# Two-block transformer kernel on one core: the second block's values are multiplied ahead of its norm, and the gates' weights follow the units

## The reference, cut to what matters

```
def rmsnorm(x, g):
    y = x * rsqrt(mean(x * x, axis=-1) + EPS)
    return y * g

h = rmsnorm(x, norm_g)
proj = h @ w_in
aq, ak, av, az, bqk, bv, bi, bf, bo, bz, ga, gb = split(proj)
q = rope(rmsnorm(two_map_heads(aq), q_norm_g), cos, sin)
k = rope(rmsnorm(two_map_heads(ak), k_norm_g), cos, sin)
v = av                                   # the attention's values
...
return x + u @ w_o                       # the x of the next layer
```

## Time and profile before

| | |
|---|---|
| median of 3 runs | 1798.98 us (1798.03 to 1799.15) |
| the profiled execution | 1797.98 us, span 1796.1 us |
| TensorE busy in the span | 1731.1 us, 96% |
| mean granted TensorE clock | 0.984 of full speed |
| VectorE, ScalarE, GpSimd busy | 63%, 51%, 26% |

### The profile page before, as it was taken

How to read it: one execution, slowest core, us unless ns; L and a number is a source line. 1 busy time by engine, 2 the same in 40 slices (tenths; PEclk the granted TensorE clock), 3 DMA queues, 4 the chain that set the end, 5 groups by cost and what they waited for, 6 DMA issues and landing times.

```text
span 1796.1 us, 29026 instructions
## 1 busy us (share of the span) xinstructions
PE 1731.1 (96%) x10836; PEld 1433.7 (80%) x10836; DVE 1127.6 (63%) x2007; ACT 924.6 (51%) x1968; POOL 459.8 (26%) x864
## 2 busy tenths in 40 slices
PE   6999998999999999988999989999999899999998
PEld 3453566888888876557999988899899898998998
DVE  4228866888878333685555577686556675785555
ACT  3237653525252523674555565575554564664542
POOL 1016001000000020320000134067771161287730
PEclk9999999999999998998999999999999999999999
DMA  9323332455555321202554443524345335433351
GB/s 341 139 94 122 135 120 94 141 187 188 188 188 188 141 74 47 95 1 94 188 187 175 171 147 124 196 99 142 136 142 187 142 107 199 144 127 141 120 193 42
DMA packets 127541, 255.28 MB, mean 142 GB/s; under 512 B 2462, under 2 KB 7212, under 8 KB 127404
## 3 DMA queue, kind: packets, MB, share of 16 engines
q1 hardware_dynamic: 126406, 251.16, 39.3%
q0 software_dynamic: 704, 2.10, 0.4%
q10 hardware_dynamic: 294, 0.18, 0.0%
HBM read 252.38 MB, written 1.05 MB: 141 GB/s over the span
## 4 chain that ended last, share of the span: by engine, by line
PE 51%; DVE 1%; ACT 1%; issue 0%; POOL 0%; DVEq 0%; ACTq 0%
PE ps L1189 12%; PE ps L1191 12%; PE ps L1190 12%; PE ps L1436 2%; PE ps L1434 2%; PE ps L1435 2%; PE ps L1514 1%; PE ps L1517 1%; PE ps L1509 1%; PE ps L1090 1%; PE ps L1063 1%; PE ps L1480 1%; PE ps L1204 0%; PE ps L1205 0%; ACT big_r L1623 0%; DVE big_r L2091 0%
## 5 line engine op out<-in xcount | busy, mean ns | idle before, releaser
L2091 DVE TENSOR_TENSOR big_r<-ring,big_r 128x1024 fp32r<-128x1024 f32 x214 | 263.9, 1233 | 249.3 <-ACT big_r L1623 249.2
L1623 ACT ACTIVATE big_r<-ring 128x1024 fp32r<-128x1024 f32 x214 | 226.2, 1058 | 370.8 <-PE ps L1191 358.3
L1190 PE MATMUL ps<-big_r 128*128 128x256 f32 (+1 forms) x1088 | 360.6, 331 | 0.0
L1189 PE MATMUL ps<-hT_r,big_r 128*128 128x256 f32 (+1 forms) x848 | 270.6, 319 | 0.0
L1191 PE MATMUL ps<-hT_r,big_r 128*128 128x256 f32 (+1 forms) x848 | 265.6, 313 | 0.0
L1189 PE MATMUL ps<-big_r 128*128 128x256 f32 (+1 forms) x720 | 239.9, 333 | 1.4 <-DVE big_r L2277 1.4
L1191 PE MATMUL ps<-big_r 128*128 128x256 f32 (+1 forms) x720 | 237.9, 330 | 0.0
L930 POOL TENSOR_TENSOR sq<-sq 128x256 f32<-128x256 f32 (+1 forms) x30 | 36.1, 1202 | 730.4 <-ACT sq L1583 730.2
L1190 PEld LDWEIGHTS ps<-big_r 128*128 128x128 f32 x1088 | 206.8, 190 | 18.7
L1191 PEld LDWEIGHTS ps<-hT_r,big_r 128*128 128x128 f32 x848 | 161.5, 190 | 9.6
L1189 PEld LDWEIGHTS ps<-hT_r,big_r 128*128 128x128 f32 x848 | 161.6, 191 | 9.3 <-issue 0.2
(11 more groups left out here) (319 smaller groups left out, 4280.7 us busy)
## 6 DMA issues: line engine op xcount, KB each, us to landing
ring<-in_w_in SPq DMA_DIRECT2D x44, 2048.0 KB, 7.7
ring<-in_w_mlp SPq DMA_DIRECT2D x32, 2048.0 KB, 7.9
ring<-in_w_mod SPq DMA_DIRECT2D x24, 2048.0 KB, 8.0
ring<-in_w_out SPq DMA_DIRECT2D x4, 2048.0 KB, 9.0
ring<-in_w_out_a SPq DMA_DIRECT2D x4, 2048.0 KB, 7.8
ring<-in_w_out_b SPq DMA_DIRECT2D x4, 2048.0 KB, 7.8
ring<-in_w_o SPq DMA_DIRECT2D x4, 2048.0 KB, 7.8
ring<-in_w_in SPq DMA_DIRECT2D x2, 1152.0 KB, 11.0
```

The lines of the kernel that those rows point to most:

```text
L1189: mm(b[:, 0:T], w_hi[:, k, :], hi(k), start=(j == 0), stop=False)
L1190: mm(b[:, 0:T], w_hi[:, k, :], lo(k), start=False, stop=False)
L1623: act_fn(hi, raw, ACT.Copy).then_inc(hi_ready, 1)
L2091: V.tensor_tensor(lo, raw, hi.bitcast(F32), ALU.subtract).then_inc(lo_ready, 1)
```

## The change

In each layer of the second block, `av` is moved from behind the units to the very start. Its left operand is no longer the normed `h` but `x * g` in two rounded parts (`g_hi` made by `gained` on ScalarE, `g_lo` by `gained_rest` on VectorE, chunk by chunk as the last product of the layer before updates `xT`). Each token's root is brought from a row to a column by two transposes on TensorE (bank key `roots`) and a small copy, and multiplies the values when ScalarE copies them out of PSUM. The sum of squares comes behind the first of the eight `av` granules, the transposes behind the fifth. The splitting of granules 3 to 7 is woven into the chunk loop of the norm on both engines. The tail behind the units is now the two granules of `bif` and the first of `bv`. The order of slots, the banks of `av` and two buffers of the granules follow. No matmul of the products is added or removed.

```
@@ plan_banks @@
     for l in range(DEPTH):
         tag = ("b", l)
+        for n in range(4):
+            take((tag, "av", n), (2 if n // 2 == l else 6) + n % 2)
         take((tag, "lam"), 5)
         take((tag, "n1"), 4)
+        take((tag, "roots"), 5)
         unit_plan(tag, units_b())
-        for n in range(4):
-            take((tag, "av", n), n)
         for n in range(4):
             take((tag, "bv", n), n)
         take((tag, "bif"), 4)
-BEFORE = ("aq", "ak", "av", "bif", "bv")
+BEFORE = (("av", 0), ("av", 1), ("aq", 0), ("aq", 1), ("ak", 0), ("ak", 1), ("bif", 0), ("bv", 0), ("bv", 1))
...
@@ TensorE @@
+                for n, m in [(n, m) for n in range(2) for m in range(4)]:
+                    if n == 0:
+                        pe.wait_ge(g_ready, KC * l + 2 * m + 2)
+                    tokens_granule("av", n, m, g_hi[l], g_lo[l])
+                    if (n, m) == (0, 0):
+                        summed_squares((tag, "n1"), SEQ)
...
+                    if (n, m) == (1, 0):
+                        key = (tag, "roots")
+                        b = start_bank(key)
+                        pe.wait_ge(nt_ready, nt_before[l] + 1)
+                        for t in range(2):
+                            last = tr(b[:, t * P:(t + 1) * P], rstd[:, root_slot[l], t * P:(t + 1) * P], IDENT)
+                        fill(last, key)
...
-                run_units(tag, units_b(), main, [lambda m=m: tokens_granule("av", 0, m) for m in range(B_BUFS)])
-                tokens_product("av", B_BUFS)
...
+                run_units(tag, units_b(), main, [lambda: gates_granule(0), lambda: gates_granule(1),
+                                                 lambda: tokens_granule("bv", 0, 0, hb1_hi, hb1_lo)])
+                tokens_product("bv", 1)
...
@@ ScalarE @@
+            def gained(l, k):
+                act_fn(g_hi[l][:, k, :], xT[:, k, LAT:TOK], ACT.Copy, scale=gain(DEPTH + l, RB["g"] + k))\
+                    .then_inc(g_hi_ready, 1)
...
                 square_summed((tag, "n1"), KC - 1, last + (KC - 1,), LAT)
-                hi_to(first_gran["b", l] + 2)
+                gained(l, KC - 1)
+                hi_to(first_gran["b", l] + 3)
                 reciprocal_root((tag, "n1"), P, SEQ, D)
-                hi_to(first_gran["b", l] + 3)
                 await_bank(act, (tag, "lam"))
                 drain(act_fn(small[:, 0:2], bank((tag, "lam"))[:, 0:2], ACT.Exp), (tag, "lam"))
                 for k in range(KC):
                     nts[0] += 1
                     act.wait_ge(nt_ready, nts[0])
+                    if k in (0, 1, 3, 5, 7):
+                        hi_to(first_gran["b", l] + 4 + (k + 1) // 2)
                     act_fn(hb1_hi[:, k, :], nt[:, k % 2, 0:SEQ], ACT.Copy).then_inc(h_hi_ready, 1)
+                await_bank(act, (tag, "roots"))
+                roots = bank((tag, "roots"))[:, 0:SEQ].rearrange("p (t q) -> p t q", t=2)[:, :, 0]
+                drain(act_fn(small[:, 20:22], roots, ACT.Copy), (tag, "roots"))
+                await_drained(act, (tag, "roots"))
+                for n in range(4):
...
+                    drain(act_fn(av_tok[:, t, half * 512:(half + 1) * 512], bank(key)[:, :], ACT.Copy,
+                                 scale=small[:, 20 + t:21 + t]), key)
+                    if n == 1:
+                        hi_to(first_gran["b", l] + 10)
+                hi_to(first_gran["b", l] + 11)
                 run_units(tag, units_b())
+                hi_to(gran_no[("bv", l, 0), 0] + 2)
...
@@ VectorE @@
+            def gained_rest(n):
+                while n_gained[0] < n:
...
+                    dve.wait_ge(g_hi_ready, n_gained[0])
+                    V.scalar_tensor_tensor(g_lo[l][:, k, :], xT[:, k, LAT:TOK], gain(DEPTH + l, RB["g"] + k),
+                                           g_hi[l][:, k, :].bitcast(F32), ALU.mult, ALU.subtract).then_inc(g_ready, 1)
...
-                lo_to(first_gran["b", l] + 2)
+                gained_rest(KC * (l + 1))
+                lo_to(first_gran["b", l] + 3)
                 n = newton((tag, "n1"), P, SEQ, D)
                 for k in range(KC + 2):
+                    if k in (1, 2, 4, 6, 8):
+                        lo_to(first_gran["b", l] + 4 + k // 2)
                     if k >= 2:
...
                     if k < KC:
...
-                lo_to(first_gran["b", l] + 3)
+                lo_to(first_gran["b", l] + 11)
...
@@ VectorE, in run_units, ahead of the last two rotations @@
-                    lo_to(gran_no[("av", tag[1], 0), 3] + B_BUFS)
+                    lo_to(gran_no[("bv", tag[1], 0), 0] + 2)
```

More of the change, by code:

```diff
@@ L361, in granules_b @@
     before = []
-    for name in BEFORE:
+    for name, n in BEFORE:
         if name == "bif":
@@ L366, in granules_b @@
             continue
[L367 to L373, removed]
+        for m in range(4):
+            if name in ("av", "bv"):
+                product = (b, name, 2 * n + 1) if m == 3 else None
+            else:
+                product = (b, f"{name}{4 * n + m}", 0)
+            before.append(((name, l, n), m, product))
     mid = [((name, l, c // 4), c % 4, (b, name, c)) for name, c in MID]
@@ L395, in plan_slots @@
     for l in range(DEPTH):
-        for name in BEFORE:
-            slots += [(name, l, n) for n in range(1 if name == "bif" else 2)]
+        slots += [(name, l, n) for name, n in BEFORE]
         slots += [(name, l, n) for name, n in MID_SLOTS]
@@ L536, in program @@
         u_hi, u_lo = over(5), xT_r[:, :, 0:SEQ]
+        g_hi, g_lo = (over(4), over(3)), (over(5), over(6))
         def pair(region):
@@ L717, in buffer_b @@
             def buffer_b(j):
-                return ("b", ("h" if j < n_before else "norms", "end" if j < n_after else "mqk", "spare")[j % B_BUFS])
+                last = "end" if j < n_after else "mqk"
+                others = ("spare", last) if l == 0 else (last, "spare")
+                return ("b", (("h" if j < n_before else "norms",) + others)[j % B_BUFS])
             phase(("b", l), before + mid + after, buffer_b)
@@ L1406, in _, with tokens_granule @@
                 tag = ("b", l)
[L1407 to L1411, removed]
+                def tokens_granule(name, n, m, x_hi, x_lo):
+                    keys = [(tag, name, 2 * n + t) for t in range(2)]
+                    banks = [start_bank(key) if m == 0 else bank(key) for key in keys]
+                    g = gran_no[(name, l, n), m]
+                    pe.wait_ge(lo_ready, g + 1)
+                    w_hi, w_lo = gran_bufs[g]
+                    for t in range(2):
+                        o = banks[t].rearrange("p (a c) -> p a c", a=4)
+                        for k in range(2):
+                            x0, x1 = (x[:, 2 * m + k, t * P:(t + 1) * P] for x in (x_hi, x_lo))
+                            y_hi, y_lo = (w[:, 4 * k:4 * k + 4, :] for w in (w_hi, w_lo))
+                            mm(o, x0, y_hi, start=(m == 0 and k == 0), stop=False)
+                            mm(o, x0, y_lo, start=False, stop=False)
+                            last = mm(o, x1, y_hi, start=False, stop=(m == 3 and k == 1))
+                        if m == 3:
+                            fill(last, keys[t])
+                    if m < 3:
+                        last.then_inc(gran_used, 1)
@@ new lines, in _ @@
+                for n, m in [(n, m) for n in range(2) for m in range(4)]:
[4 more added lines that the diff above has]
+                        summed_squares((tag, "n1"), SEQ)
+                        key = (tag, "lam")
+                        b = start_bank(key)
+                        pe.wait_ge(lam_prod, l + 1)
+                        fill(mm(b[:, 0:2], cc("ones", HD), small[0:HD, 16:18], start=True, stop=True), key)
+                    if (n, m) == (1, 0):
+                        key = (tag, "roots")
+                        b = start_bank(key)
+                        pe.wait_ge(nt_ready, nt_before[l] + 1)
+                        for t in range(2):
+                            last = tr(b[:, t * P:(t + 1) * P], rstd[:, root_slot[l], t * P:(t + 1) * P], IDENT)
+                        fill(last, key)
@@ L1420, in main @@
                         split_product(gran_of[(tag, name, 0)], h_hi_at, h_lo_at, SEQ)
[L1422 to L1440, removed]
                 def tokens_product(name, first=0):
                     for g in range(first, 8):
-                        tokens_granule(name, g // 4, g % 4)
+                        tokens_granule(name, g // 4, g % 4, hb1_hi, hb1_lo)
                 def features_product(name, hi, lo, first=0):
@@ L1448, in features_product, with gates_granule @@
                         split_product(gran_of[(tag, name, c)], hi, lo, SEQ)
-                run_units(tag, units_b(), main, [lambda m=m: tokens_granule("av", 0, m) for m in range(B_BUFS)])
-                tokens_product("av", B_BUFS)
-                key = (tag, "bif")
-                b = start_bank(key)
-                for g in range(2):
+                def gates_granule(g):
```

(4 more changed lines are left out.)

34 lines of the change are left out of this document (23 added, 11 removed).

## The result

On one chip, in turns with the kernel before, the changed kernel took 1802.54 us (median of 13 runs, 1799.81 to 1804.66) where the kernel before took 1798.67 (13 runs, 1796.02 to 1800.93): a ratio of 1.0022, 95% interval 1.0015 to 1.0030, or 3.9 us more. The same kernel once more on another occasion gave 1.0018 (1.0009 to 1.0027), 3.2 us more. That is just at the bound of 0.2% that the prediction names. The forecast was 1803.5 in 1799.5 to 1807.0, with +4.5 us as its sum.

The account below looks back on a forecast made before the run. TensorE, busy 96% of the span, was taken as the bound. -4.1 (start) + 6.2 (both waits) + 2.4 (clock) = +4.5 us on 1797.98 gives 1802.5, and 1803.5 as median; range 1799.5 to 1807.

Parts of the forecast that it names:

- the gates' wait: Ahead of `bif` in each layer: TensorE idle 2.6 us until unit 14's Newton instruction drains bank 4.
- the stalls of the start: At each layer's start: TensorE idle 1.2 to 1.4 us each ahead of `av` granules 5, 6, 7 and `aq0`.
- the second wait: Ahead of `bv`'s fifth granule: gate instructions start some 1 us later against the product, 0.5 us lost a layer.
- The start: From the layer before to the end of `aq0` and `aq1`, both layers: 4.1 us saved, bounds 1 to 7.
- The turns: In the norm's chunk loop: ScalarE and VectorE alternate instead of working side by side, 4.07 us a granule against TensorE's 2.73.
- a better weaving: At each layer's start: one hidden turn a granule would gain another 1.5 us; much better weaving shares a 0.1 chance.
- The clock: Around the gates' granules: the idle gap lowers TensorE's granted clock in some places, 1.2 us a place, 2.4 in all.
- the likeliest case: Whole kernel: both waits come and the clock falls at one place or both, 1801.5 to 1806.5 us; chance 0.5.
- the rival in which the clock holds: At the gates: the wait comes but the clock stays up, +2.1 us, 1801.1, inside 0.2%; chance 0.3.
- the hidden wait: At `bif`: Newton done when TensorE arrives, 1795.9 us or 1793; chance 0.1, shared with much better weaving.
- fall in the stalls of the start: At the layers' starts: the clock falls in the 1.3 us stalls too, some 3 us each, 1809; chance 0.1.

Follow-up runs that it names:

- e2_fill: Changed kernel with 20 extra matmuls, read by nobody, ahead of the gates' first granule: 1801.38 us, ratio 1.0020; again 1800.36 us, 1.0020.
- e1_bank: Changed kernel with the gates' product moved from PSUM bank 4 to bank 0 and `bv`'s banks to 1, 4, 2, 3: 1795.24 us, ratio 0.9984.
- e3_weave: Changed kernel, ScalarE rounding the next granule before it waits for the next `nt`, not behind it: 1795.22 us, ratio 0.9988 to the kernel before.
- g_weave: The kernel of `e3_weave` once more, on one chip with `g_weave_fill`: 1794.14 us, ratio 0.9983 to the kernel before.
- g_weave_fill: The kernel of `e3_weave` with the 20 extra matmuls of `e2_fill` ahead of the gates: 1792.89 us, ratio 0.9974 to the kernel before.
- e4_both: Changed kernel with the banks of `e1_bank` and the order of `e3_weave` together: 1787.30 us, ratio 0.9941 to the kernel before.
- e5_three: `e4_both` plus ScalarE rounding `bv`'s fifth granule before it waits for VectorE's gates: 1786.14 us, ratio 0.9931 to the kernel before.
- e5_again: The kernel of `e5_three` once more, beside others on one chip: 1784.19 us, ratio 0.9929 to the kernel before.
- e6_later: Changed kernel with `bv`'s first granule ahead of the gates' two granules, gates still in bank 4: 1798.06 us, ratio 1.0001.

## Why the prediction held

The layer's length by kernel, in us:

| kernel | length | what it lacks against the changed kernel |
|---|---|---|
| before | 377.33 | |
| changed | 380.31, 380.28 | |
| `e2_fill`, twice | 378.80, 378.83 | the fall of the clock |
| `e1_bank` | 376.16 | the clock's fall and the gates' wait |
| `e3_weave`, `g_weave` | 376.43, 376.41 | the stalls of the start |
| `g_weave_fill` | 374.92 | those and the clock's fall |
| `e4_both` | 372.34 | the gates' wait too |
| `e5_three`, `e5_again` | 371.50, 371.50 | the second wait too |
| `e6_later` | 377.47 | the clock's fall and the gates' wait, for a longer second wait |

They add up from either side. The gates' wait is worth 378.82 - 376.16 = 2.66 without the new weaving and 374.92 - 372.34 = 2.58 with it; the weaving 3.88, 3.90 and 3.82 (380.30 - 376.42, 378.82 - 374.92, 376.16 - 372.34).

**The start** (forecast -4.1). Right: 1.8 and 2.65 us, 4.5 in all. The turns came as worked out, 4.07 us a granule, and with them the end of `aq0` and `aq1` at 33.81 and 33.69 instead of 33.95. TensorE starts granules 5, 6 and 7 and `aq0` 15.84, 19.90, 23.97 and 27.99 us behind the layer before, where the forecast has 16.0, 20.0, 24.1 and 28.2. The stalls ahead of granules 6 and 7 cost 1.33 and 1.34 us, inside the forecast's 1.2 to 1.4, though the profile's idle shows only 0.9 to 1.05. Only the one ahead of granule 5 is smaller than that, 0.27 and 0.33 us of idle; the forecast's own times (granule 4 ends at 15.0, two transposes, granule 5 at 16.0) leave no 1.2 there either. That the order of two lines makes them was then shown by `e3_weave`, in which they went. The forecast's bound for a better weaving, 1.5 a place, was too small: with the order turned round it was 3.8 to 3.9.

**The gates' wait** (forecast 2.6 a layer, bounds 2.4 and 2.8). Right in place, releaser and size: idle 2.35 and 2.36, a shade under the lower bound as the profile counts idle, and worth 2.71 from matmul to matmul and 2.58 to 2.66 in the layer's length. The sum behind the forecast's number is not quite right: its own rows give 1100.40 + 0.1 - 1097.75 = 2.75 and not 2.6, and the 2.71 came out next to that. `e1_bank` shows the cause: the same product at the same place in another bank doesn't wait.

**The second wait** (forecast 0.5 a layer, 0 to 0.8). Right in its chain, too small in its size. The last gate instruction, ScalarE's rounding and TensorE's last matmul before it stood still, changed kernel:

```profile
1134.64 0.41 DVE L2391 TENSOR_TENSOR w_uq_sb<-w_uq_sb 8x256 f32<-8x256 f32 x1
1137.36 1.06 ACT L1645 ACTIVATE hT_r<-ring 128x1024 fp32r<-128x1024 f32 x1
1138.88 0.39 PE L1428 MATMUL ps<-big_r,xT_r 128*128 128x512 f32 x1
```

The rounding comes 2.72 us behind the gate instruction, as before. The gate instruction stands 1.3 us later against the product, where the forecast has some 1. The idle is 0.56 and 0.51 us, but from start to start the wait takes 0.79 (1138.88 to 1139.83 and the slower first matmul behind it, against 0.23 a matmul) and 0.76, and its removal was worth 0.84. So the sum should have had 1.6 for it, not 1.0.

**The clock** (forecast 2.4 for two places, bounds 0 and 2.3 a place). The fall came where the forecast has it, behind the gates' gap and not in the stalls of the start, which left the granted clock at 1.00. Its size is 1.49 us a fall, against 1.2 taken for each place between bounds of 0 and 2.3. It fell in one of the two places in both profiles of the changed kernel, so 1.5 us of the 2.4 were there. How often it falls in runs without a profile isn't shown: the medians with and without the extra matmuls are 0.1 us apart in one pair on the same chip and 1.25 in the other, and each interval reaches 1.6 or more to each side. The Trainium skill ("TensorE: Matmul & The Clock Gate", section "Why this matters for your kernels") asks only that no idle gap between bursts is longer than about 3 us; the prediction set this rule against the term. It does not hold here: gaps of 2.35 and 2.36 us were followed by the lower level in six of the eight places in four profiles (the changed kernel twice, `e3_weave`, `g_weave`), and the 1.49 us are its price. Nor does the gap alone decide, since two of the eight held at 1.00.

**The sum.** -4.5 + 2 x 2.66 + 1.6 + 1.5 = +3.9 us, against 3.8 from the block's start to the end of the profiled span and 3.9 and 3.2 in the medians. The forecast of +4.5 was 0.6 above that sum: 0.9 too much by the clock's second place and 0.4 by the start, 0.7 too little by the two waits. The mechanism was right, but a part of the closeness is luck: 1.3 us too much stood against 0.7 too little. And whether the total is told from no change at all hangs on 0.2%, so between the likeliest case and the rival in which the clock holds (+2.1) the traces decide and not the time: the clock fell in one place of two, and that is the likeliest case, at its lower edge. Against the rivals: the hidden wait did not come, since Newton is as late as it was (2.47 and 2.48 us behind the mean squares); the clock did not hold in every place; and it did not fall in the stalls of the start. No experiment took the gates' move back alone, with the old place of that product; what stands for it is `e1_bank`, in which the move is there and its wait isn't.

## What to carry to other kernels

A product that is moved forward takes its bank with it: before moving it, ask who drained that bank last at the new place, and how late. Here that one assignment, with the fall of the clock behind it, made the difference between a gain of about 0.2% and a loss of 0.2%. Where two engines prepare work for a third, look at the order in which each takes its waits: an engine that waits for a partner before it does what the partner needs makes turns out of what could go side by side, and here turning two lines round gave back 3.8 to 3.9 us a layer. And where run-to-run noise is as large as the effect, measure a stretch between two fixed instructions in the profiles, which here repeated to 0.03 us. And take the cost of a wait from start to start: the idle that the profile shows was 0.23 to 0.36 us less than the cost in each of the three kinds of wait.

## What the hardware showed that was not expected

- Equal gaps, unequal clocks: behind an idle of 2.35 or 2.36 us between dense stretches the granted clock fell to the lower level in six places, between 0.2 us before and 0.8 us after TensorE began again, and stayed there for 3.4 us each time; in two places it held at 1.00. Behind the waits of 2.09 and 2.10 us of `e6_later` it fell once and held once. Gaps of about 1.0 us, three of them with 8.1 us from the first one's end to the last one's, left it at 1.00 each time.
- A fall costs the same each time, 1.45 to 1.51 us.
- Matmuls whose result nobody reads held the clock, in all six places where they were put, and cost nothing as they fit into the gap: 20 of them, 2.71 us, and the gates started 2.95 us behind the mean squares with them and without.
